# Scores of two heads at once in row tiles, several query blocks per group, in a two-network forward pass

## The chip, the cores and the metric

The kernel runs on one core of a Trainium2 chip. The metric is the device time of one execution in microseconds (us), as the median of several runs. Beside it there is one profiled execution, from which all durations come. Engines are named as in the profile: PE is TensorE's matmul, PEld its weight load, DVE is VectorE, ACT is ScalarE, POOL is GpSimd, SP issues most of the transfers; a "q" behind a name (SPq, ACTq) is the instruction queue of that engine.

## The reference, cut to what matters

A sequence of 512 tokens with 1024 features goes through two networks, one after the other. All data are fp32. Three attentions lie in it, each followed by an output projection and a feed-forward part:

```python
# 1. forgetting attention: 8 heads of 64 features
logits = einsum('bhqd,bhkd->bhqk', qf, kf) + c[q] - c[k]      # c: running sum of log gates
logits = where(key <= query, logits, -inf)                    # causal
# 2. differential attention: 8 heads, each with two maps over 64 features
sc = einsum('bqhcd,bkhcd->bhcqk', q, k) * scale
p = masked_softmax(sc, key // 64 <= query // 64)              # in chunks of 64
a = p[:, :, 0] - lam * p[:, :, 1]
# 3. latent attention: 16 heads, scores over 64 + 32 = 96 features
proj = h @ w_in                                               # 384 + 256 + 32 columns
sc = (einsum(q_nope, k_nope) + einsum(q_pe, k_pe)) * scale    # same chunk mask
```

## The kernel before

**Arithmetic.** Every fp32 operand is split into a high and a low part of type fp32r, and each product is three matmuls: high by high, low by high (or high by low), and the other. The weights stream from memory in chunks of up to 1024 columns per partition (`RAW`), are split by ACT (`WH`, L1990) and DVE (`WL`, L1809), and are used at once. A chunk feeds 12 to 24 matmuls.

**Order of the work.** The kernel is written as many small generators ("strands") that yield steps. A planner at build time gives each step an estimated duration (`takes`) and picks, engine by engine, the step that can begin first, with some patience for more urgent ones. The order it finds is fixed in the program; on the chip each engine runs its own list and waits on semaphores. So a change of the estimates or of the steps can move work on every engine. PSUM has eight banks; `cap["gemm"]` and `cap["one"]` say how many of them projections and attention steps may hold.

**Scores.** A query block is 128 queries; block i sees (i + 1) * 128 keys. In the forgetting attention ("fg") and the latent attention ("mla") one step `score` computes one head and one block in one bank: three matmuls over the keys (L1747 to L1749), for "fg" a fourth one that adds the gates (L1752), and one of 128 columns that adds the mask in the last 128 keys (L1753, operands in `RC`). In "fg" two heads lie in one 128-row tile of Q, rows 0 to 63 and rows 64 to 127. The step uses all 128 rows: the keys of a head stand in their own tile of `KT` whose other half was zeroed at the start (`k_zero`, L2121). In "mla" the matmuls over the keys use 96 rows, the mask matmul all 128:

```python
mask = (IDR, MASK_C) if kind == "fg" else (HALF, MASK_H)
...
e.matmul(dst[:, nk - P:nk], *st.mask, start=False, stop=True)   # L1753
```

In the differential attention ("da") one step `score_two` computes the two maps of one head and one block in two banks. Its matmuls use 64 rows each, rows 0 to 63 for one map and rows 64 to 127 for the other, in turn (L1761), and two mask matmuls of 64 rows (L1763). After each score come `max` (DVE, L1870), `exp` (ACT, L2068), the division (DVE, L1876 or its "da" form), the transposes on PE (`turn`, L1664), their split into `PT` (ACT L1994, DVE L1815), and one `value` step per head (L1659 to L1661).

**Gates of "fg".** `gate_rows` issues four small transfers on SP (L1635), from `R` to `FS`, which place the eight heads' gate rows on partitions; ACT then copies them (`gate_cq`, L2086) and makes a selected row set for each head (`key_row`, L2064). On SP the next weight chunk stands behind these transfers (L1596).

**Latent projection.** `w_in` of the latent attention has 672 columns. They are computed in two passes over eight k-tiles and four token tiles, of 512 and 160 columns (L1688 to L1690).

Of the kernel before, what the change touches and what calls it, by code (L numbers as in the profile page):

```python
# [5 lines left out]
P = 128  # L6
S = 512
# [12 lines left out]
C_ID, C_MA, C_MC, C_IH, C_ONE = 0, 128, 256, 384, 512  # L20
C_SEL = 640
C_BASE = 648
C_CDA, C_SDA = 650, 682
C_CML, C_SML = 714, 778
C_WF = 842
C_END = 906
# [7 lines left out]
STN = 8  # L34
# [9 lines left out]
    "vec": {"pe": 1, "act": 1}, "cvec": {"pe": 1, "act": 1}, "consts": {"act": 1}, "k_zero": {"pool": 1}, "blank": {"pool": 1},  # L44
# [5 lines left out]
    "key_row": {"act": 1}, "score": {"pe": 1}, "score_two": {"pe": 1}, "max": {"dve": 1}, "exp": {"act": 1},  # L50
# [87 lines left out]
def takes(kind, eng, f):  # L138
# [9 lines left out]
    if eng == "pe":  # L148
# [48 lines left out]
    return {"acc": 1595.0, "window": 1250.0, "kpe_copy": 1130.0, "k_zero": 520.0, "ramp": 220.0}.get(kind, 120.0)  # L197


def build(nc, a, out):  # L200
    with ExitStack() as ctx:
# [11 lines left out]
        RC = sb("RC", [P, 512], F32R)  # L213
# [17 lines left out]

        IDR, MASK_C, MASK_H, HALF = (RC[:, n * P:n * P + P] for n in range(4))

# [22 lines left out]
        strands, ready_at, free_at = [], {}, dict.fromkeys(LAG, 0.0)  # L256
# [7 lines left out]
        def emit(kind, **fields):  # L264
            t = None
            for eng, n in SIGNALS[kind].items():
# [33 lines left out]
        def run():  # L300
            while strands:
# [22 lines left out]
                s = min((x for x in can if x[1] == eng and x[0] <= t + PATIENCE[eng]), key=lambda x: x[2].rank)[2]  # L324
# [402 lines left out]
        def landing(s, t):  # L727
# [7 lines left out]
        k_zeros = [emit("k_zero", lo=64 if hh % 2 == 0 else 0, i=s * 8 + hh * 2 + x).pool  # L735
                   for s in range(2) for hh in range(4) for x in range(2)]
        kfree = [[k_zeros[-1]] for _ in range(16)]
# [105 lines left out]
        def k_tiles(base):  # L843
            def put(n, bank, done):
                parts, his = [(base + (2 * n + x) * 2, slice(64 * x, 64 * x + 64)) for x in (0, 1)], []
                for i, r in parts:
                    st = yield step("hi", dst=KT[r, i, :], src=bank[r, :], scale=1.0, after=counts([done, kfree[i], kfree[i + 1]]))
                    his.append(st.act)
                for (i, r), hi in zip(parts, his):
                    st = yield step("lo", dst=KT[r, i + 1, :], src=bank[r, :], high=KT[r, i, :], scale=None, from_x=False, after=[hi])  # L850
                    kready[i] = [st.dve]
                return [st.dve]
            return put

# [10 lines left out]
        def attention(groups, kind, lag):  # L865
            nh = 2 if kind == "da" else 4
            krows = 96 if kind == "mla" else P
            mask = (IDR, MASK_C) if kind == "fg" else (HALF, MASK_H)
            units = [(G, h, i) for G in groups for h in range(nh) for i in range(4)]
# [4 lines left out]
            def key_rows(G, h, u):  # L874
                while u > state.scored + 2 or not (flags.consts and G.gated) or not tiles.fr:
                    yield None
# [1344 lines left out]
```

## Time and profile before

| | |
|---|---|
| runs | 1829.54, 1827.6, 1829.36 us; median 1829.36 us |
| the profiled execution, its own time | 1828.21 us |
| its span (first to last instruction) | 1826.4 us |
| granted TensorE clock, mean | 1.00 |
| PE busy | 1808.6 us (99%) |
| PEld busy | 1494.4 us (82%) |
| DVE busy | 1121.5 us (61%) |
| ACT busy | 799.3 us (44%) |
| POOL busy | 145.2 us (8%) |

The duration of a matmul in the profile is from its start to its modelled end, and matmuls overlap in it; what one costs in a stream is the distance to the start of the next one. "Idle before" counts only time in which no record of the engine is open. The forgetting attention lies at about 68 to 150 us of the span, the differential one at 618 to 800 us, the latent projection and attention at 1220 to 1440 us; the rest is projections and feed-forward parts.

### The profile page before, as it was taken

The numbers are of one execution on the slowest core, as the hardware profiler recorded it, in microseconds if no ns is written. First come the engines' busy times: TensorE is split into PE (matmuls) and PEld (weight loads), VectorE is DVE, ScalarE is ACT, GpSimd is POOL, SyncE is SP. The second block draws the span as 40 slices with busy tenths as digits, with TensorE's granted clock in tenths as the row PEclk, the third lists the DMA queues.
The fourth block names the chain that finished last, engine by engine and source line by source line (L and its number), as shares of the span: only waits on it lengthen the run. The fifth ranks groups of instructions, "written<-read, shape, count | busy, mean of one in ns | idle before, by whom it ended". The sixth has DMA issues, their size and how long they took to land.

```text
span 1826.4 us, 23160 instructions
## 1 busy us (share of the span) xinstructions
PE 1808.6 (99%) x8960; PEld 1494.4 (82%) x8960; DVE 1121.5 (61%) x1898; ACT 799.3 (44%) x1426; POOL 145.2 (8%) x149
## 2 busy tenths in 40 slices
PE   9999999999999999999999999999999999999998
PEld 7898788888888888888888888779888888888886
DVE  5577644344345777696754654655989776366375
ACT  6562432122235455544432433447766544144144
POOL 4003200000004100002000000024000100000000
PEclk9999999999999999999999999999999999999999
DMA  5212323322332211213323333222011233332331
GB/s 160 71 36 67 105 92 93 92 93 93 100 96 92 70 59 61 68 58 93 93 93 92 93 93 99 92 79 73 26 58 36 59 93 97 99 93 93 92 117 68
DMA packets 128251, 152.24 MB, mean 83 GB/s; under 512 B 9291, under 2 KB 100973, under 8 KB 128141
## 3 DMA queue, kind: packets, MB, share of 16 engines
q1 hardware_dynamic: 127980, 150.69, 26.8%
q8 instruction: 71, 1.16, 0.3%
q14 instruction: 40, 0.32, 0.1%
q10 hardware_dynamic: 160, 0.07, 0.0%
HBM read 148.56 MB, written 2.10 MB: 82 GB/s over the span
## 4 chain that ended last, share of the span: by engine, by line
PE 92%; DVE 3%; issue 1%; ACT 1%; POOL 1%; DMA 0%; SPq 0%; DVEq 0%; POOLq 0%; ACTq 0%
PE bk L1659 22%; PE bk L1661 22%; PE bk L1660 22%; PE bk L1688 6%; PE bk L1689 5%; PE bk L1690 5%; PE bk L1664 4%; PE bk L1761 1%; PE bk L1747 1%; PE bk L1749 1%; PE bk L1748 1%; PE bk L1726 1%; DVE XT L1821 1%; PE bk L1733 1%; POOL FS L2130 1%
## 5 line engine op out<-in xcount | busy, mean ns | idle before, releaser
L1659 PE MATMUL bk<-R,WH 128*128 128x512 f32 x1764 | 700.6, 397 | 1.8 <-DVE R L1799 1.3
L1660 PE MATMUL bk<-R,WH 128*128 128x512 f32 x1764 | 696.7, 395 | 0.0
L1661 PE MATMUL bk<-R,WL 128*128 128x512 f32 x1764 | 696.7, 395 | 0.0
L1809 DVE TENSOR_TENSOR WL<-RAW,WH 128x1024 fp32r<-128x1024 f32 (+4 forms) x277 | 341.1, 1232 | 529.3 <-ACT WH L1990 527.8
L1990 ACT ACTIVATE WH<-RAW 128x1024 fp32r<-128x1024 f32 (+4 forms) x277 | 287.9, 1039 | 651.6 <-PE bk L1661 593.0
L1659 PEld LDWEIGHTS bk<-R,WH 128*128 128x128 f32 x1764 | 330.8, 188 | 81.7 <-issue 2.9
L1661 PEld LDWEIGHTS bk<-R,WL 128*128 128x128 f32 x1764 | 330.6, 187 | 80.9
L1660 PEld LDWEIGHTS bk<-R,WH 128*128 128x128 f32 x1764 | 330.8, 188 | 78.7
L1688 PE MATMUL bk<-WH,R 128*128 128x512 f32 (+4 forms) x528 | 187.8, 356 | 0.0
L1689 PE MATMUL bk<-WH,R 128*128 128x512 f32 (+4 forms) x528 | 180.2, 341 | 0.0
L1690 PE MATMUL bk<-WL,R 128*128 128x512 f32 (+4 forms) x528 | 180.1, 341 | 0.0
L2130 POOL TENSOR_TENSOR FS<-FS 128x512 f32<-128x512 f32 x49 | 75.4, 1549 | 910.0 <-ACT FS L2014 908.2
L1799 DVE SCALAR_TENSOR_TENSOR FS<-FS,VEC 128x511 f32<-128x511 f32 (+1 forms) x176 | 125.1, 747 | 7.8 <-ACT FS L2096 7.0
L1821 DVE TENSOR_TENSOR XT<-bk,XT 128x512 f32<-128x512 f32 x152 | 100.8, 684 | 25.7 <-PE bk L1661 25.4
L1688 PEld LDWEIGHTS bk<-WH,R 128*128 128x128 f32 x528 | 99.7, 189 | 11.4 <-issue 1.0
L1690 PEld LDWEIGHTS bk<-WL,R 128*128 128x128 f32 x528 | 99.4, 188 | 11.5
L1689 PEld LDWEIGHTS bk<-WH,R 128*128 128x128 f32 x528 | 99.7, 189 | 9.2
L2068 ACT ACTIVATE FS<-bk,SM 128x128 f32<-128x128 f32 (+3 forms) x160 | 83.5, 526 | 52.6 <-DVE SM L1870 52.1
L1910 DVE TENSOR_TENSOR FS<-bk,FS 128x512 f32<-128x512 f32 x136 | 90.2, 685 | 11.1 <-PE bk L1661 9.6
L2096 ACT ACTIVATE FS<-FS,VEC 128x512 f32<-128x512 f32 x88 | 69.0, 810 | 52.7 <-DVE FS L1910 52.7
L1870 DVE TENSOR_REDUCE SM<-bk 128x1 f32<-128x128 f32 (+3 forms) x160 | 72.8, 482 | 6.0 <-PE bk L1753 5.0
L1994 ACT ACTIVATE R<-FS 128x512 fp32r<-128x512 f32 x78 | 47.5, 623 | 63.4 <-DVE FS L1922 43.1
(153 smaller groups left out, 1676.3 us busy)
## 6 DMA issues: line engine op xcount, KB each, us to landing
RAW<-in_ffn_w_up_dram SPq DMA_DIRECT2D x176, 256.0 KB, 3.1
RAW<-in_ffn_w_down_dram SPq DMA_DIRECT2D x44, 512.0 KB, 3.7
RAW<-in_w_gate_dram SPq DMA_DIRECT2D x44, 256.0 KB, 2.9
RAW<-in_w_up_dram SPq DMA_DIRECT2D x44, 256.0 KB, 3.1
RAW<-in_w_down_dram SPq DMA_DIRECT2D x22, 512.0 KB, 3.6
RAW<-in_da_w_qkv_dram SPq DMA_DIRECT2D x32, 256.0 KB, 3.0
RAW<-in_w_out_dram SPq DMA_DIRECT2D x8, 512.0 KB, 3.7
RAW<-in_da_w_qkv_dram SPq DMA_DIRECT2D x8, 512.0 KB, 3.5
```

The costliest lines, as they stand in the source:

```text
L1659: e.matmul(dst, lh, rh, start=start, stop=False)
L1660: e.matmul(dst, lh, rl, start=False, stop=False)
L1661: return e.matmul(dst, ll, rh, start=False, stop=stop)
L1688: e.matmul(dst, R[:, xh, t], wh[:, j, :], start=st.start and j == 0, stop=False)
L1689: e.matmul(dst, R[:, xl, t], wh[:, j, :], start=False, stop=False)
L1690: mm = e.matmul(dst, R[:, xh, t], wl[:, j, :], start=False, stop=st.stop and j == top)
L1799: return e.scalar_tensor_tensor(out=dst, in0=x, scalar=s, in1=y, op0=o0, op1=o1)
L1809: e.tensor_tensor(low, RAW[:, r, 0:m], high.bitcast(F32), ALU.subtract).then_inc(on["wlo_dve"], 1)
L1821: e.tensor_tensor(XT[:, st.m, :], BK[st.bank][:, :], XT[:, st.m, :], ALU.add).then_inc(on["add_dve"], 1)
L1910: e.tensor_tensor(st.dst, BK[st.bank][:, :], st.bc, ALU.mult).then_inc(on["scaled_dve"], 1)
L1990: e.activation(home(st.n)[0], RAW[:, r, 0:m], ACT.Copy).then_inc(on["whi_act"], 1)
L2130: e.tensor_tensor(st.acc, st.acc, st.x, ALU.add).then_inc(on["acc_pool"], 1)
```

## The change

1. **One step `pair` replaces `score` of "fg" and `score_two` of "da".** It handles two heads of "fg" (or two maps of a "da" head) and one or more query blocks. All its matmuls use 64 rows, the two halves in turn, each into its own bank. In "fg" the keys of two heads now share one tile, as in "da" (`k_pair` instead of `k_tiles`), so the zeroing of `KT` is gone.
2. **Several blocks in one step** (`bundles`). In "fg" blocks 0 and 1 share a step and a bank per half, blocks 2 and 3 are steps of their own. In "da" blocks 0 and 1 likewise, and blocks 2 and 3 are one step with four banks.
3. **Masks.** `RC` holds `MASK_C`, `MASK_H` and a shifted identity that is read as `UPPER` and `LOWER`. In "fg" the causal mask needs two matmuls per half (one of 128 and one of 64 columns) instead of one. In "mla" the mask matmul uses rows 0 to 63 alone, where it used 128.
4. **Gates.** `gate_rows` issues eight transfers instead of four, since the gate rows are wanted on both halves; `key_row` runs once per pair of heads.
5. **The planner** adds 195 ns to an estimate where PE goes from `pair` to anything else or back, and prefers a further `pair` step right after one. Nothing is added for the mask of "mla".
6. **Latent projection** in passes of 384 and 288 columns; the transposes of its first three tiles wait for the first pass alone.
7. **Banks in "da"**: `cap["gemm"]` is 4 instead of 5. The lag of "da" (how many blocks the scores may be ahead) is 2 instead of 3.

The core of the diff:

```diff
-        if kind == "score":
-            return (3 if f["gate"] is None else 4) * mm((f["i"] + 1) * P) + 62
-        if kind == "score_two":
-            return 3 * max(220.0, 1.1 * mm((f["i"] + 1) * P)) + 200
+        if kind == "score":
+            return 3 * mm((f["i"] + 1) * P) + 62
+        if kind == "pair":
+            return sum((3 if f["gate"] is None else 4) * mm((i + 1) * P) + (60 if f["gate"] is None else 120) for i, _, _ in f["parts"])
...
+                    if eng == "pe" and (kind == "pair") != tiled[0]:
+                        t += 195.0
+                        tiled[0] = kind == "pair"
...
-            chunk(2, 512, (0, wap(m_in, k * P, 2, 0, 512)))
-        for k in (0, 4):
-            chunk(4, 160, (0, wap(m_in, k * P, 4, 512, 160)))
+            chunk(2, 384, (0, wap(m_in, k * P, 2, 0, 384)))
+        for k, n in ((0, 3), (3, 3), (6, 2)):
+            chunk(n, 288, (0, wap(m_in, k * P, n, 384, 288)))
...
-        k_zeros = [emit("k_zero", lo=64 if hh % 2 == 0 else 0, i=s * 8 + hh * 2 + x).pool
-                   for s in range(2) for hh in range(4) for x in range(2)]
...
-            attention([A0, A1], "fg", 2)
+            paired([A0, A1], "fg", 2, ([[0, 1]], [[2]], [[3]]))
...
-            cap["gemm"] = 5
-            attention(Gs, "da", 3)
+            cap["gemm"], cap["one"] = 4, 4
+            paired(Gs, "da", 2, ([[0, 1]], [[2], [3]]))
...
                     for r0, src, dst in st.rows:
                         e.dma_start(FS[r0:29 + r0:4, dst, 0:S], R[0:8, src, :].bitcast(F32)).then_inc(s_c, 16)
+                        e.dma_start(FS[64 + r0:93 + r0:4, dst, 0:S], R[0:8, src, :].bitcast(F32)).then_inc(s_c, 16)
...
-                    e.matmul(dst[:, nk - P:nk], *st.mask, start=False, stop=True).then_inc(on["score_pe"], 1)
+                    e.matmul(dst[:, nk - P:nk], UPPER[0:64, :], MASK_H[0:64, :], start=False, stop=True).then_inc(on["score_pe"], 1)
+                elif k == "pair":
+                    sides = (slice(0, 64), slice(64, 128))
+                    for i, o, bs in st.parts:
+                        nk, q = (i + 1) * P, slice(i * P, i * P + P)
+                        two = [(r, BK[b][:, o:o + nk]) for r, b in zip(sides, bs)]
+                        for x, y in ((0, 0), (1, 0), (0, 1)):
+                            for r, dst in two:
+                                e.matmul(dst, R[r, st.q[x], q], KT[r, st.kidx + y, 0:nk], start=x == y, stop=False)
+                        if st.gate is None:
+                            for r, dst in two:
+                                mm = e.matmul(dst[:, nk - P:nk], UPPER[r, :], MASK_H[r, :], start=False, stop=True)
+                        else:
+                            cq, ck = st.gate
+                            for r, dst in two:
+                                e.matmul(dst, R[r, cq, q], R[r, ck, 0:nk], start=False, stop=False)
+                            for r, dst in two:
+                                e.matmul(dst[:, nk - P:nk], UPPER[r, :], MASK_C[r, :], start=False, stop=False)
+                            for r, dst in two:
+                                mm = e.matmul(dst[:, nk - 64:nk], LOWER[r, :], MASK_C[r, 0:64], start=False, stop=True)
```

**Where the change moves instructions.** On PE the first scores of "fg" stand behind the same projection matmuls as before. Before (L1747 to L1749 keys, L1752 gates, L1753 mask, all of 128 rows; "128x128" is output partitions by columns):

```order
L1690 MATMUL bk5<-WL,R 128x512
L1747 MATMUL bk4<-KT,R 128x128 [waits key_row_act,gate_cq_act,tok_f_act,lo_dve]
L1748 MATMUL bk4<-KT,R 128x128
L1749 MATMUL bk4<-KT,R 128x128
L1752 MATMUL bk4<-R 128x128
L1753 MATMUL bk4<-RC 128x128
L1747 MATMUL bk1<-KT,R 128x256 [waits tok_f_act,lo_dve]
```

The same place now (L1848 keys, L1855 gates, L1857 and L1859 masks, all of 64 rows):

```order
L1778 MATMUL bk5<-WL,R 128x512
L1848 MATMUL bk4<-KT,R 128x128 [waits tok_f_act,key_row_act,lo_dve,gate_cq_act]
L1848 MATMUL bk1<-KT,R 128x128
L1848 MATMUL bk4<-KT,R 128x128
L1848 MATMUL bk1<-KT,R 128x128
L1848 MATMUL bk4<-KT,R 128x128
L1848 MATMUL bk1<-KT,R 128x128
L1855 MATMUL bk4<-R 128x128
L1855 MATMUL bk1<-R 128x128
L1857 MATMUL bk4<-RC 128x128
L1857 MATMUL bk1<-RC 128x128
L1859 MATMUL bk4<-RC 128x64
```

Two heads are computed where one was, and the first of these matmuls waits for the same two ACT steps. On PE in the latent attention, one block before (L1688 to L1690 are projection matmuls):

```order
L1747 MATMUL bk2<-KT,R 128x256 [waits lo_dve]
L1748 MATMUL bk2<-KT,R 128x256
L1749 MATMUL bk2<-KT,R 128x256
L1753 MATMUL bk2<-RC 128x128
L1688 MATMUL bk6<-WH,R 128x512 [waits lo_dve,tok_k_act]
```

and the first two blocks of a head now (L1835 to L1837 keys with 96 rows, L1838 mask with 64 rows):

```order
L1778 MATMUL bk6<-WL,R 128x384
L1835 MATMUL bk5<-KT,R 128x128 [waits lo_dve]
L1836 MATMUL bk5<-KT,R 128x128
L1837 MATMUL bk5<-KT,R 128x128
L1838 MATMUL bk5<-RC 128x128
L1835 MATMUL bk1<-KT,R 128x256 [waits lo_dve]
L1836 MATMUL bk1<-KT,R 128x256
L1837 MATMUL bk1<-KT,R 128x256
L1838 MATMUL bk1<-RC 128x128
```

A mask matmul still closes each block, 64 times in all, each between matmuls of 96 or 128 rows. On SP, where the gate rows are placed, before:

```order
L1596 DMA RAW<-in_w_in_dram 128x4x256 [waits wlo_dve]
L1635 DMA FS<-R 8x512 [waits gate_base_dve,lo_dve]
L1635 DMA FS<-R 8x512 x3
L1596 DMA RAW<-in_w_in_dram 128x4x256 [waits wlo_dve]
```

and now:

```order
L1683 DMA RAW<-in_w_in_dram 128x4x256 [waits wlo_dve]
L1722 DMA FS<-R 8x512 [waits gate_base_dve,lo_dve]
L1723 DMA FS<-R 8x512
L1722 DMA FS<-R 8x512
L1723 DMA FS<-R 8x512
L1722 DMA FS<-R 8x512
L1723 DMA FS<-R 8x512
L1722 DMA FS<-R 8x512
L1723 DMA FS<-R 8x512
L1683 DMA RAW<-in_w_in_dram 128x4x256 [waits wlo_dve]
```

Four transfers have come in ahead of the next weight chunk and of what ACT waits for.

Counted over the whole order of PE, unbroken runs of 64-row matmuls number 24 before, all in "da". Now there are 16 in "da", 10 in "fg" (two of the twelve steps follow another one directly) and 64 in "mla", these of one matmul each.

## Rows read from the trace of the kernel before

**Rows 1.** The page: span and busy time of PE.

```profile
span 1826.4 us, 23160 instructions
...
PE 1808.6 (99%) x8960; PEld 1494.4 (82%) x8960; DVE 1121.5 (61%) x1898; ACT 799.3 (44%) x1426; POOL 145.2 (8%) x149
```

**Rows 2.** Busy time by engine, first half of the latent attention; PEclk is the granted clock.

```profile
1262.00:1345.00 83.00, 79.98 (x497) 70.47 (x496) 71.47 (x171) 55.78 (x144) 14.19 (x20) 1.00 0.13 39
```

**Rows 3.** PE in order of time (start us, us), projections of 264 and 512 columns.

```profile
51.23 0.28 PE L1689 MATMUL bk<-WH,R 128*128 128x264 f32 x1
51.34 0.28 PE L1690 MATMUL bk<-WL,R 128*128 128x264 f32 x1
51.47 0.40 PE L1688 MATMUL bk<-WH,R 128*128 128x512 f32 x1
51.70 0.40 PE L1689 MATMUL bk<-WH,R 128*128 128x512 f32 x1
```

**Rows 4.** PE in order of time, latent projection, pass of 160 columns.

```profile
1233.82 0.27 PE L1689 MATMUL bk<-WH,R 128*128 128x160 f32 x1
1233.93 0.28 PE L1690 MATMUL bk<-WL,R 128*128 128x160 f32 x1
```

**Rows 5.** PE in order of time, a score of the forgetting attention: gates, mask.

```profile
73.19 0.27 PE L1752 MATMUL bk<-R 128*128 128x128 f32 x1
73.30 0.28 PE L1753 MATMUL bk<-RC 128*128 128x128 f32 x1
```

**Rows 6.** PE in order of time, differential attention: into and out of 64 rows.

```profile
618.28 0.28 PE L1689 MATMUL bk<-WH,R 128*128 128x256 f32 x1
618.40 0.28 PE L1690 MATMUL bk<-WL,R 128*128 128x256 f32 x1
618.65 0.55 PE L1761 MATMUL bk<-KT,R 64*128 64x128 f32 x6
...
619.52 0.26 PE L1763 MATMUL bk<-RC 64*128 64x128 f32 x2
619.71 0.39 PE L1688 MATMUL bk<-WH,R 128*128 128x256 f32 x1
619.94 0.28 PE L1689 MATMUL bk<-WH,R 128*128 128x256 f32 x1
```

**Rows 7.** Weight loads in order of time at the same place.

```profile
618.62 0.44 PEld L1761 LDWEIGHTS bk<-KT,R 64*128 64x128 f32 x6
...
619.71 0.19 PEld L1688 LDWEIGHTS bk<-WH,R 128*128 128x128 f32 x1
619.82 0.19 PEld L1689 LDWEIGHTS bk<-WH,R 128*128 128x128 f32 x1
```

**Rows 8.** PE in order of time, latent attention: a mask, then a block of 384.

```profile
1298.12 0.22 PE L1753 MATMUL bk<-RC 128*128 128x128 f32 x1
...
1298.41 0.34 PE L1748 MATMUL bk<-KT,R 96*128 96x384 f32 x1
1298.59 0.34 PE L1749 MATMUL bk<-KT,R 96*128 96x384 f32 x1
```

**Rows 9.** Weight loads at the same place: the two behind that mask's.

```profile
1298.13 0.19 PEld L1747 LDWEIGHTS bk<-KT,R 96*128 96x128 f32 x1
1298.24 0.19 PEld L1748 LDWEIGHTS bk<-KT,R 96*128 96x128 f32 x1
```

**Rows 10.** SP's queue in order of time: the gate rows.

```profile
60.31 2.75 SPq L1635 DMA_DIRECT2D FS<-R  x4
```

**Rows 11.** ACT in order of time: gate copy, weight split, key rows.

```profile
64.46 0.63 ACT L2086 ACTIVATE R<-FS 128x512 fp32r<-128x512 f32 x1 [3.62 <-DMA FS<-R]
65.38 1.06 ACT L1990 ACTIVATE WH<-RAW 128x1024 fp32r<-128x1024 f32 x1 [0.29 <-PE bk L1690]
66.34 1.32 ACT L2064 ACTIVATE R<-FS,CN 128x512 fp32r<-128x512 f32 x2
```

**Rows 12.** PE in order of time: the first score of all.

```profile
67.92 0.22 PE L1747 MATMUL bk<-KT,R 128*128 128x128 f32 x1
```

More of the change, by code:

```diff
@@ L323, in run @@
                 t, eng, _ = min(can, key=lambda x: (x[0], x[2].rank))
-                s = min((x for x in can if x[1] == eng and x[0] <= t + PATIENCE[eng]), key=lambda x: x[2].rank)[2]
+                more = [x for x in can if eng == "pe" and tiled[0] and x[2].next[0] == "pair" and x[0] <= t + 200.0]
+                s = min(more or (x for x in can if x[1] == eng and x[0] <= t + PATIENCE[eng]), key=lambda x: x[2].rank)[2]
                 kind, fields = s.next
@@ L841, in k_pair @@
             return put
[L843 to L853, printed above, removed]
         def k_tiles64(base):
@@ L870, in attention @@
+        def attention(groups, lag):
+            units = [(G, h, i) for G in groups for h in range(4) for i in range(4)]
             state = Group()
@@ L872, in attention, with unit @@
             state.halves = {}
-            def key_rows(G, h, u):
-                while u > state.scored + 2 or not (flags.consts and G.gated) or not tiles.fr:
-                    yield None
-                ck = tiles.get()
-                st = yield step("key_row", dst=R[:, ck.i, :], src=G.ck, head=G.h0 + h, after=counts([ck.free, G.ck_done]))
-                ck.ready = [st.act]
-                G.ckh[h] = ck
-            def one_map(L, u, c, b, scored):
+            def unit(u):
                 G, h, i = units[u]
                 nk, o = (i + 1) * P, u % STN * 8
-                nm, z = ST[:, o + c:o + c + 1], ST[:, o + 2 + c:o + 3 + c]
-                mx = yield step("max", dst=nm, src=BK[b.i][:, 0:nk], after=[scored])
+                while state.scored < u or u > state.turned + lag or not (G.turned and flags.consts and h < G.heads):
+                    yield None
+                nm, z, rz = (ST[:, o + x:o + x + 1] for x in (0, 2, 4))
+                b = yield from bank()
+                q, kidx = G.Q[h], G.kbase + 2 * h
+                st = yield step("score", bank=b.i, q=(q.h.i, q.l.i), kidx=kidx, i=i, rows=96,
+                                after=counts([b.free, q.ready, kready[kidx]]))
+                state.scored = u + 1
+                if i == 3:
+                    drop(q, st.pe)
+                mx = yield step("max", dst=nm, src=BK[b.i][:, 0:nk], after=[st.pe])
                 p = yield from fslot()
@@ L942, in unit @@
+                st = yield step("p_one", z=z, rz=rz, p=FS[:, p.i, 0:nk], after=[ex.act])
                 odd = h % 2
@@ L976, in values @@
                         drop(v, st.pe)
[L977 to L1006 removed]
+                yield from half_out(G, pair, odd, b, st.pe)
             for G in groups:
[L1009 to L1012 removed]
+                G.undone = 4
             for n in range(len(units) // 4):
@@ L1333, in turn_lat @@
             b = yield from bank()
-            st = yield step("heads", bank=b.i, c0=f * P, width=P, after=counts([b.free, lat.toks[0:4 if f < 4 else 8]]))
+            st = yield step("heads", bank=b.i, c0=f * P, width=P, after=counts([b.free, lat.toks[n - 4:n]]))
             lat.ups.append(st.pe)
```

352 lines of the change are left out of this document (207 added, 145 removed).

## The prediction

> **What bounds the kernel now.** I read the page first: PE is busy 1808.6 of 1826.4 us, and no other engine comes near [rows 1]. So the time is the length of PE's list plus its waits, and almost every edit has to be priced in PE time. A matmul's duration says little for that, since matmuls overlap; I read in the timeline of PE how far apart the starts of two neighbours are, and call it the slot. It is 0.23 us for 512 columns and 0.12 for 264 [rows 3], 0.12 for 256 [rows 6], 0.18 for 384 (0.175 over many) [rows 8], and 0.11 for 160 [rows 4] and for 128 [rows 5]. So below some 250 columns a slot is 0.11 us whatever its columns: the weight load takes that long. The clock granted is 1.00 (the 2.4 GHz level) [rows 2], and the slots hold at it.
>
> Second, the places where 64-row matmuls begin and end, since the change makes more of them. In an unbroken stream the next weight load starts together with the running matmul: behind the mask that starts at 1298.12 it starts at 1298.13 [rows 8, 9]. At 618.40 a 256-column matmul starts, the last of 128 rows; its stream is over 0.12 later, at 618.52. The first 64-row load starts only at 618.62 [rows 6, 7]. At the other end the last 64-row mask starts at 619.56 (a pair, the second 0.04 behind the 619.52), streams for 0.06 until 619.62, and the next 128-row load starts at 619.71, 0.09 later; its matmul is recorded with 0.39 us instead of 0.28 and its neighbour starts 0.23 behind it instead of 0.12. So at each crossing PE runs empty (0.10 and 0.09) and then shows the whole load (0.11). In: 0.21 us. Out: 0.20 us. As a check, from 618.40 to 619.94 are 1.54 us; the slots in it are two of 256 columns (0.24), five pairs at 0.11 and three at 0.12 (0.91): 1.15, and 0.39 is left for one way in and out.
>
> Third, what a pair costs. With 0.41 us for the two crossings by the loads, the eight pairs between them get 0.89, 0.11 each: a pair costs what a single matmul of its columns costs.
>
> **The change part by part, in PE time.**
>
> *Forgetting attention.* Before, a head is four blocks of four matmuls and a mask: 5 x 0.11, 4 x 0.12 + 0.11, 4 x 0.175 + 0.11, 4 x 0.233 + 0.11, together 3.0 us, 23.9 for eight heads. Now four pairs of heads: blocks of four pairs and two mask pairs, 0.67 + 0.69 + 0.92 + 1.15 = 3.4 us, 13.7 in all, and ten runs of 64 rows at 0.39: 17.6. Saved: 6.3 us.
>
> *Differential attention.* The same matmuls, but 16 runs for 24: 8 x 0.39 = 3.1 us saved.
>
> *Latent projection.* 96 matmuls of 512 and 96 of 160 become 96 of 384 and 96 of 288. 288 lies between 264 (0.12) and 384 (0.175), by a straight line at 0.132. Saved per pair 0.233 + 0.112 - 0.175 - 0.132 = 0.038, times 96: 3.6 us.
>
> *Masks of the latent attention.* This edit looks like nothing, and I take it for the largest. There are 64 of them, each now a single 64-row matmul between 96- or 128-row ones. From the end of the stream ahead to the start of the next matmul it takes in (0.21), stream (0.06), out (0.20): 0.47 us. Now it takes one slot of 0.11: load to load 1298.13 to 1298.24 [rows 9]. So 0.35 more, times 64: 22.4 us lost. The trace has no single one, so both ends: if the loads could still run ahead and only the emptying stays, 0.10 + 0.06 + 0.09 - 0.11 = 0.14 (9 us); if a single one costs its slot and the full 0.39, 25 us. Nothing at all is a rival below. I take 0.35, since in [rows 6, 7] both halves of the price show at both crossings.
>
> On this, the Trainium skill, TensorEngine Tiling (Array Packing), Key Properties, says that changing the tiling mode, not just the tile, drains TensorE. It gives no number; the gaps of 0.10 and 0.09 in [rows 7] agree with it, and the exposed load is what the trace adds. It speaks against this edit. Another page would have it the other way: the Trainium skill, TensorE: Matmul & The Clock Gate, Step-by-step: what each phase is for, has weight loads pulled ahead of running matmuls where they go to the background buffer. By it the masks would cost nothing and the sum would be 22 us lower, as in rival one.
>
> *Gates.* Four transfers are issued in 2.75 us [rows 10]; eight take 2.7 us more. ACT waits for them (3.62 us idle already), then splits a weight chunk and makes the key rows [rows 11]: the first is done 0.66 after 66.34, at 67.00. PE reads it at 67.92 [rows 12], after the same matmuls as now. The 2.7 us shrink by the 0.29 that ACT then waited for PE; the first key row comes at 69.4, and PE stands still for 1.5 us. Behind it in PE's list is all the rest. Ends: 1.0 and 2.5. The weight chunk behind the transfers on SP comes 2.7 us late too; a chunk feeds 24 matmuls of 0.233, 5.6 us, and three are split ahead, so it costs nothing; without that cover it would add up to 2.7.
>
> *At nothing:* the zeroing of the keys (POOL, at the very start, long before a key tile is read); fewer key splits on ACT and DVE in the first attention (both have idle time there); one bank less for projections in the differential part (a bank is read out while three others still compute; uncovered it would be one copy of 0.63 us as in [rows 11] for each of eight projections, 5 us).
>
> *What is absorbed.* In 1262 to 1345 PE is idle 3.0 of 83 us while DVE is busy 71.5 [rows 2]. Idle counts only what exceeds the 0.28 us tail of the last matmul, so up to twice that is waiting. There half the masks lie, and PE's longer list gives DVE the time it lacked. I take 3 us, between 0 and 6.
>
> **Sum.** -6.3 - 3.1 - 3.6 + 22.4 + 1.5 - 3.0 = +7.9 us against the profiled execution: its span would be 1834.3 and its own time 1836.1. The median of the runs stands 1.15 above that execution's own 1828.21, so I predict 1837 for the median.
>
> **The rivals.** 0.2% is 3.7 us, about what a measurement can tell from no change.
>
> *One: a single 64-row matmul at rows 0 to 63 crosses free.* Then only the savings and the gate stall are left: -13.0 + 1.5 = -11.5, 1818 us, faster. For it: no such matmul is in the trace. Against it: every crossing there is shows both parts. It decides the sign when a mask costs under (11.5 - 3)/64 = 0.13 us, with nothing absorbed under 0.18. Chance 0.11.
>
> *Two: a part of the price.* The loads run ahead (0.14 each, 9 us) or the absorption is at its end of 6 us: 9 - 11.5 = -2.5 in the one case, 22.4 - 11.5 - 6 = +4.9 in the other; between them 1826 to 1833. For it: DVE at 86% busy in half the masks' stretch. Against: an absorption of 6 needs twice the waiting that the rows show. Chance 0.14, of it 0.04 faster and 0.10 the same.
>
> *Three: bursts that starve.* A two-group step of the differential part needs all four attention banks at once, and a transpose behind it waits until an exp gives one back; the scores are now ahead by two blocks instead of three. Eight such steps, each late by one copy of 0.63 us [rows 11], add 5 us to the forecast: 1842. Against: projections stand between the steps in the order. Chance 0.07.
>
> *The forecast,* the masks at about 0.35: 0.68, its own range 1833 to 1843 (0.30 to 0.39 a mask, the absorption 0 to 6).
>
> **How the numbers follow.** Forecast, two and three together hold 0.89, and the range 1826 to 1844 covers about 0.8 of the whole; rival one lies outside. Faster: 0.11 + 0.04 = 0.15. Same: 0.10 of rival two and 0.03 of the forecast's lower end, 0.13. Slower: the rest, 0.72.
>
> **What would show it.** In the trace of the changed kernel: around each latent mask (L1838) its weight load should start 0.1 us after the stream ahead is over, not with it, and the next matmul's load about 0.25 us after the mask's, with a duration 0.1 longer; if the loads stay 0.11 apart, rival one holds. The stretch of the latent attention should be some 19 us longer, the first one 5 us shorter with its gate stall, the differential one 3 shorter, and the first `pair` should start near 69.4 with PE idle before it. PE's total idle should stay under 20 us; if it grows by 5 in the differential part, rival three holds. The prediction fails if a mask costs under 0.2 us, or if the new order makes waits that the old trace can't show.

## The result: 1.0% faster, where 0.4% slower was predicted

| | median of the runs | lowest to highest |
|---|---|---|
| before, run beside it | 1829.45 us (4 runs) | 1827.6 to 1830.07 |
| changed kernel | 1811.14 us (4 runs) | 1809.0 to 1812.49 |

The ratio is 0.9901, 95% interval 0.9883 to 0.9918. The predicted 1837 us and its range (1826 to 1844) lie above it. One execution of one kernel below (everything 32 bytes on) fell into a slower state, 1969.9 us at a granted clock of 0.85, and is left out of its median.

The page of the changed kernel, for [rows 1]:

```profile
span 1810.7 us, 23164 instructions
...
PE 1785.5 (99%) x8992; PEld 1496.8 (83%) x8992; DVE 1120.2 (62%) x1895; ACT 791.7 (44%) x1419; POOL 136.1 (8%) x133
```

PE is busy 23.1 us less, but it has 32 matmuls more, and it stands idle 25.2 us where it was 17.8 (the prediction wanted under 20 as a sign). So the time came from matmuls that cost less, not from fewer waits. To see which, I looked first where the change does nothing. Between 300 and 400 us of the span there are only feed-forward matmuls of 512 columns, before and after. These are the windows of PE there (stretch, length, busy and number of matmuls, granted clock, DMA share, GB/s), of the kernel before:

```profile
300.00:400.00 100.00, 100.00 (x430) 1.00 0.31 94
```

and of the changed one:

```profile
300.00:400.00 100.00, 100.00 (x442) 1.00 0.33 98
```

The same clock, no idle time, and 12 matmuls more in 100 us. PE in order of time shows it from matmul to matmul (start, duration in us), before:

```profile
299.95 0.39 PE L1660 MATMUL bk<-R,WH 128*128 128x512 f32 x1
300.18 0.40 PE L1661 MATMUL bk<-R,WL 128*128 128x512 f32 x1
300.42 0.39 PE L1659 MATMUL bk<-R,WH 128*128 128x512 f32 x1
300.65 0.40 PE L1660 MATMUL bk<-R,WH 128*128 128x512 f32 x1
```

and after:

```profile
300.05 0.39 PE L1748 MATMUL bk<-R,WH 128*128 128x512 f32 x1
300.27 0.39 PE L1749 MATMUL bk<-R,WL 128*128 128x512 f32 x1
300.50 0.39 PE L1747 MATMUL bk<-R,WH 128*128 128x512 f32 x1
300.73 0.39 PE L1748 MATMUL bk<-R,WH 128*128 128x512 f32 x1
```

Three slots took 0.70 us and take 0.68. Over the 100 us (one of the counted matmuls reaches in from before) that is 0.2331 and 0.2268 us a slot. The kernel has three groups of 1764 matmuls of 512 columns that read `R` and the weights (`WH` or `WL`), 5292 in all, so 5292 x 0.0063 = 33 us. The prediction had counted this slot as fixed.

**What the change itself did** can be read where the prediction said. A mask of the latent attention, in PE's order of time:

```profile
1245.86 0.28 PE L1837 MATMUL bk<-KT,R 96*128 96x256 f32 x1
1246.07 0.32 PE L1838 MATMUL bk<-RC 64*128 64x128 f32 x1
1246.32 0.44 PE L1835 MATMUL bk<-KT,R 96*128 96x384 f32 x1
1246.60 0.33 PE L1836 MATMUL bk<-KT,R 96*128 96x384 f32 x1
```

The weight loads at the same place:

```profile
1245.74 0.19 PEld L1837 LDWEIGHTS bk<-KT,R 96*128 96x128 f32 x1
1246.07 0.18 PEld L1838 LDWEIGHTS bk<-RC 64*128 64x128 f32 x1
1246.32 0.19 PEld L1835 LDWEIGHTS bk<-KT,R 96*128 96x128 f32 x1
```

The stream of the 256 columns is over at 1245.98, the mask's load starts 0.09 later (forecast 0.1), the next load 0.25 behind that one (forecast 0.25), and the matmul behind it is recorded with 0.44 instead of 0.34 [rows 8]. From 1245.86 to 1246.60 are 0.74 us. With a mask that costs its slot it would be 0.12 + 0.11 + 0.175 = 0.405, so the mask costs 0.335 more, times 64: 21.4 us (predicted 22.4).

The gates of the forgetting attention, in PE's order:

```profile
67.27 0.39 PE L1778 MATMUL bk<-WL,R 128*128 128x512 f32 x1
69.34 0.55 PE L1848 MATMUL bk<-KT,R 64*128 64x128 f32 x6 [1.69 <-ACT R L2160]
```

and the first and last of the eight transfers on SP's queue:

```profile
60.14 0.74 SPq L1722 DMA_DIRECT2D FS<-R  x1
...
64.93 0.62 SPq L1723 DMA_DIRECT2D FS<-R  x1
```

They end at 65.55, 2.5 us behind the four of [rows 10] (63.06), and the first pair starts at 69.34 (predicted 69.4) with PE idle for 1.69 us (predicted 1.5). Against [rows 12] that is 1.42 us later.

**Two things are new in this trace.** The waits of PE by line and releaser (us in total, times, longest), the costliest ones:

```profile
PE bk L1747 <- DVE R L1911: 3.1, 2, 2.3
PE bk L1752 <- ACT TOK L2146: 2.6, 1, 2.6
PE bk L1747 <- DVE R L1895: 2.2, 2, 2.0
```

And three stretches in which the granted clock is at its lower level, 1.2 GHz. One of them, in windows of PE:

```profile
575.00:578.00 3.00, 2.05 (x14) 1.00 0.41 140
578.00:585.00 7.00, 7.00 (x22) 0.51 0.24 75
```

The same in order of time:

```profile
577.01 2.49 PE L1814 MATMUL bk<-CN,FS 128*128 128x1 f32 x16 [0.95 <-POOL FS L2223]
...
579.93 0.63 PE L1777 MATMUL bk<-WH,R 128*128 128x512 f32 x1
580.36 0.63 PE L1778 MATMUL bk<-WL,R 128*128 128x512 f32 x1
```

PE had been idle for 0.95 us and then worked on sixteen matmuls of a single column; from 578 to 585 us the clock is 0.51 and matmuls of 512 columns start 0.43 us apart. The kernel before has 1.00 in the same windows. The two others lie at 816.9 us (behind an idle time of 2.26) and near 1301.8. They cost 3.4, 1.7 and 1.7 us (length times the missing share of the clock), 6.8 together. In the kernel before the granted clock is 1.00 up to its last 2 us.

### The profile page after: what moved, and what is told of

Read it like the earlier page. It is cut to its first block, busy times and chain, and to the rows that moved or that the text cites. A ratio compares the mean times of both kernels' runs of the same rounds, so it can differ in the third digit from the quotient of the medians.

```text
span 1810.7 us, 23164 instructions
## 1 busy us (share of the span) xinstructions
PE 1785.5 (99%) x8992; PEld 1496.8 (83%) x8992; DVE 1120.2 (62%) x1895; ACT 791.7 (44%) x1419; POOL 136.1 (8%) x133
## 4 chain that ended last, share of the span: by engine, by line
PE 91%; DVE 3%; ACT 2%; issue 2%; POOL 1%; DMA 0%; SPq 0%; DVEq 0%; POOLq 0%; ACTq 0%
PE bk L1747 22%; PE bk L1748 22%; PE bk L1749 22%; PE bk L1776 5%; PE bk L1778 5%; PE bk L1777 5%; PE bk L1752 4%; PE bk L1848 1%; PE bk L1838 1%; PE bk L1814 1%; POOL FS L2223 1%; DVE XT L1917 1%; PE bk L1835 1%; PE bk L1821 1%; PE bk L1836 1%
## 5 line engine op out<-in xcount | busy, mean ns | idle before, releaser
L1747 PE MATMUL bk<-R,WH 128*128 128x512 f32 x1764 | 693.2, 393 | 5.6 <-DVE R L1911 3.1
L1749 PE MATMUL bk<-R,WL 128*128 128x512 f32 x1764 | 688.6, 390 | 0.0
L1748 PE MATMUL bk<-R,WH 128*128 128x512 f32 x1764 | 688.3, 390 | 0.0
L1747 PEld LDWEIGHTS bk<-R,WH 128*128 128x128 f32 x1764 | 332.1, 188 | 75.0 <-issue 6.2
L1749 PEld LDWEIGHTS bk<-R,WL 128*128 128x128 f32 x1764 | 332.0, 188 | 69.7
L1966 DVE TENSOR_REDUCE SM<-bk 128x1 f32<-128x128 f32 (+3 forms) x160 | 71.2, 482 | 12.6 <-PE bk L1838 6.1
```

What stands on the lines that cost most here:

```text
L1747: e.matmul(dst, lh, rh, start=start, stop=False)
L1748: e.matmul(dst, lh, rl, start=False, stop=False)
L1749: return e.matmul(dst, ll, rh, start=False, stop=stop)
```

## Experiments: where the slot comes from

**Theory.** The change makes `RC` 64 columns narrower (256 bytes of a partition) and `CN` 60 columns wider (240 bytes). Tensors lie one behind the other, at starts that are rounded to 32 bytes, so all that lies behind `RC` moves down by 32 bytes against the weights. `R`, the other operand of nearly all matmuls, began 61728 bytes behind `WH`, and begins 61696 bytes behind it now. The lines that do it:

```diff
-C_END = 906
+C_END = 966
...
-        RC = sb("RC", [P, 512], F32R)
+        RC = sb("RC", [P, 448], F32R)
```

The theory: the distance of the two operands sets the slot. Rival A: something in the changed order (DMA, DVE, POOL) makes PE's stream faster. Rival B: not the distance counts but where `R` itself begins. All kernels below ran beside the kernel before on the same chip; its medians there were 1829.5 to 1830.1 us, so a comparison across the sections can be off by 0.6 us.

**Kernel before, 32 bytes more.** Only an unused tensor is added:

```diff
         RC = sb("RC", [P, 512], F32R)
+        PAD = sb("PAD", [P, 8], F32)
         VEC = sb("VEC", [P, V_END], F32)
```

> The kernel before with nothing but an unused tensor of 32 bytes per partition ahead of VEC, so that R, KT, PT and FS begin at a multiple of 64 bytes of their partition, as they do in the changed kernel (in the kernel before they begin 32 bytes past one). No instruction and no order changes. Theory A, placement: the 512-column slot of the projections falls from 0.2333 us to 0.2267 as in the changed kernel, some 6350 slots x 0.0066 = 42 us less PE time, partly given back in waits at stage borders, where PE is now ahead of the others: 1785 to 1800 us. Theory B, the new order of the instructions or less traffic by the other engines made the slots shorter: nothing changes, 1829 us and 0.2333.

Measured: 1807.11 us, ratio 0.9879 (0.9865 to 0.9892). An unused tensor is worth more than the whole change. Its windows:

```profile
300.00:400.00 100.00, 100.00 (x439) 1.00 0.31 95
```

439, a slot of 0.228, not quite that of the changed kernel, and the time lies above the 1785 to 1800 us that were expected. Rival A has fallen: no instruction and no order changed. But a start at a multiple of 64 bytes isn't the whole rule.

**Changed kernel, the old distance** (the same line added there, so that `R` is 61728 bytes from `WH` again).

> The changed kernel with an unused tensor of 32 bytes ahead of VEC, so that R, KT, PT and FS begin 32 bytes past a multiple of 64, as in the kernel before. No instruction changes. Theory A: the slot goes back to 0.2333 and the time is that of the change alone, which my sum puts 8 us over the kernel before: 1833 to 1841 us. Theory B: 1811 us and 0.2267.

Measured: 1842.71 us, ratio 1.0073 (1.0059 to 1.0087):

```profile
300.00:400.00 100.00, 100.00 (x430) 1.00 0.30 95
```

With the old slot back, the change makes the kernel slower, by 12.6 us.

**Changed kernel, everything 32 bytes on** (the unused tensor stands ahead of `XT`, the first of all: `R` and `WH` both move, their distance does not).

> The changed kernel with an unused tensor of 32 bytes ahead of everything, so that the split weights (WH, WL) and the activations (R, KT, PT) all begin 32 bytes past a multiple of 64; the distance of R from WH is a multiple of 128 bytes, as in the changed kernel, where both begin at one. Theory A1, the distance of the two operands of a matmul modulo 128 counts: slots of 0.227 us, 1811 us. Theory A2, the place of R alone counts: 0.2333 as with R moved alone, about 1842 us.

Measured: 1812.23 us, ratio 0.9908 (0.9893 to 0.9923), as the changed kernel. Rival B has fallen, by the time alone; the slot of this kernel isn't read.

**Changed kernel, weights moved instead of `R`** (32 bytes ahead of `WH` and `WL`, 32 more ahead of `VEC`: `R` moves by 64, the distance is 61728).

> The changed kernel with WH and WL 32 bytes further and R, KT and PT 64 bytes further, so R begins at a multiple of 64 bytes as in the kernel before with 32 bytes added (slot 0.229), but stands 32 modulo 128 from WH, as in the kernel before (slot 0.2333). Theory A1: 0.2333 and about 1842 us. Theory A2: 0.229 and about 1825 us.

Measured: 1841.87 us, ratio 1.0065 (1.0053 to 1.0078), and 430 matmuls in the window. That is the time of the second kernel of this section (1842.71): two ways to the same distance give the same time. And `R` begins here where it does in the first one (1807.11), so its own start doesn't set the slot.

**Kernel before, 96 bytes more** (the unused tensor of the first experiment with 24 columns).

> The kernel before with an unused tensor of 96 bytes ahead of VEC: R begins 0 modulo 128 from WH, as in the changed kernel. By theory A1 its slot is 0.227 us, 0.0065 less than before over some 6350 slots, 41 us less PE time; some 10 us of it may come back in waits and clock at stage borders: 1788 to 1800 us. It is also the fair partner of the changed kernel: the difference between them is the worth of the change without the placement, which I put at +8 and which the pair with R at 32 gave as +12.6.

Measured: 1823.68 us, ratio 0.9968 (0.9956 to 0.998):

```profile
300.00:400.00 100.00, 100.00 (x432) 1.00 0.30 94
```

1788 to 1800 us were expected. So a distance that is a multiple of 128 bytes isn't enough, and my rule was wrong. What fits all runs so far is the distance modulo 256: 61824 is 128 there.

**Kernel before, 224 bytes more,** to test that rule where it predicts and to give the changed kernel a fair partner (56 columns, distance 61952, 0 modulo 256).

> The kernel before with one edit, an unused tensor of 224 bytes per partition ahead of VEC, so that R begins 61952 bytes behind WH, 0 modulo 256 like in the changed kernel. Theory, the distance modulo 256 sets the slot: slot of 512 columns 0.227 us instead of 0.233 as in the changed kernel, and a time under the 1807 of the kernel with 64 bytes, near 1795 to 1805, if the engines behind PE keep up; then the changed kernel's own edits cost 6 to 16 us at equal placement. Rival, it is not the distance but the size of the shift (32 bytes less was good, 32 more was good, 96 more was not): then 0.233 and 1829 again. Second rival, distance counts modulo 512 (the changed kernel's 61696 is 256 modulo 512, this one's is 0): then any slot but 0.227.

Measured: 1796.03 us, ratio 0.9828 (0.9814 to 0.9841):

```profile
300.00:400.00 100.00, 100.00 (x443) 1.00 0.31 96
```

The rule held where it was tried, and both its rivals fell: 61696 and 61952 differ by 256 and give the same slot. That pair alone shows the period.

| distance R - WH, modulo 256 | kernels | matmuls in 300 to 400 us | median, us |
|---|---|---|---|
| 0 | changed; before + 224 bytes | 442; 443 | 1811.14; 1796.03 |
| 32 | before; changed + 32 bytes | 430; 430 | 1829.45; 1842.71 |
| 64 | before + 32 bytes | 439 | 1807.11 |
| 128 | before + 96 bytes | 432 | 1823.68 |

**The same within one trace.** Behind `R` lie `KT` and `PT`, and their distances to it are multiples of 256 bytes in every kernel here. The kernel before keeps the weights of its last projection there. PE in order of time:

```profile
1789.80 0.39 PE L1689 MATMUL bk<-KT,R 128*128 128x512 f32 x1
1790.03 0.39 PE L1690 MATMUL bk<-KT,R 128*128 128x512 f32 x1
1790.26 0.39 PE L1688 MATMUL bk<-KT,R 128*128 128x512 f32 x1
1790.48 0.39 PE L1689 MATMUL bk<-KT,R 128*128 128x512 f32 x1
```

Three slots take 0.68 us here, as in the changed kernel, where `WH` and `R` take 0.70 in this same kernel. Over the whole trace the median distance between two neighbours is 227 ns for `KT` with `R` (76 of them) and 234 for `R` with `WH` (1731). In the changed kernel both are 227, and with 32 bytes more there (where `R` moves and `KT` with it) they are 227 and 234 again. So it is the pair of tensors that counts, within one kernel too.

The distance table also tells what the change is worth. At distance 32 it costs 12.6 us (against the kernel before in the same section) to 13.3 us (by the table's medians), at distance 0 it costs 15.1. The placement gives 33.4 us to the kernel before and 31.6 to the changed one.

## Experiments: the parts of the change

**The mask alone, in the kernel before** (rows 0 to 63 in the latent attention, nothing else).

```diff
-                    e.matmul(dst[:, nk - P:nk], *st.mask, start=False, stop=True).then_inc(on["score_pe"], 1)
+                    mask = st.mask if st.rows == P else tuple(m[0:64, :] for m in st.mask)
+                    e.matmul(dst[:, nk - P:nk], *mask, start=False, stop=True).then_inc(on["score_pe"], 1)
```

> The kernel before with one edit of the change alone: the mask matmul of the latent attention on rows 0 to 63. By the sum +22 us of PE time less up to 6 us that the waits of that stretch absorb: 1845 to 1852 us. If the price is only the emptying, 0.14 us each: 1832 to 1838.

Measured: 1846.56 us, ratio 1.0096 (1.0082 to 1.011), 16.5 us more.

**The changed kernel with the old mask:**

```diff
-                    e.matmul(dst[:, nk - P:nk], UPPER[0:64, :], MASK_H[0:64, :], start=False, stop=True).then_inc(on["score_pe"], 1)
+                    e.matmul(dst[:, nk - P:nk], UPPER, MASK_H, start=False, stop=True).then_inc(on["score_pe"], 1)
```

> The changed kernel with the mask matmul of the latent attention on 128 rows again (the same sum twice over: the masked places get a number twice as far below, the others none). By the sum 64 masks at 0.35 us are 22 us of PE time, so 1789 us, or up to 8 us more where PE then waits for the others instead. If a single 64-row matmul were cheap in truth and the loads seen around it were only recorded late: 1811, no change.

Measured: 1794.95 us, ratio 0.981 (0.9797 to 0.9824), 16.2 us less than the changed kernel. This one edit taken back makes a faster kernel than the change was.

**All but the mask, at the old distance** (the last edit and the 32 bytes).

> The changed kernel with the latent mask on 128 rows and 32 unused bytes ahead of VEC, so that R is 61728 bytes from WH (32 modulo 256), as in the kernel before: all edits but the mask's, at the old placement. The prediction's sum without masks and absorption is -6.3 - 3.1 - 3.6 + 1.5 = -11.5: about 1818. Rival, from the runs so far: grouping blocks gave 3 us where 6 were reckoned, and the changed kernel at this distance was 12.6 over the kernel before where the mask alone gave 16.5, so the other edits together give only 4 us: 1825. At 1825 the savings are eaten by new waits and half-clock stretches, at 1818 the masks cost more beside the other edits than alone.

Measured: 1823.03 us, ratio 0.9969 (0.9959 to 0.9979). The prediction's sum for this was 1818. Against the changed kernel at that distance (1842.71) the masks are worth 19.7 us here. The mask's line in that one (64 rows), weight loads and matmuls (count: shortest/median/longest in ns):

```profile
L1839 PEld LDWEIGHTS bk<-RC x64: 182/183/183, 1266.6 to 1437.6; 64*128 64x128 f32 x64
L1839 PE MATMUL bk<-RC x64: 322/324/326, 1266.6 to 1437.6; 64*128 64x128 f32 x64
```

and with 128 rows:

```profile
L1839 PEld LDWEIGHTS bk<-RC x64: 187/188/193, 1267.2 to 1420.8; 128*128 128x128 f32 x64
L1839 PE MATMUL bk<-RC x64: 222/226/278, 1267.2 to 1421.0; 128*128 128x128 f32 x64
```

From the first mask to the last are 171.0 us with 64 rows and 153.6 with 128 (the loads' rows), 17.4 us for the 64 of them, and not one of them is spared: the shortest matmul is recorded with 322 ns. Before 32 of the 64 loads the load engine stood idle, 9.8 us in all, and the profile shows nothing that it waited for. Of the 21.4 us 4.0 were absorbed here.

**One block to a step** (in the changed kernel, 42 runs of 64-row matmuls in the first two attentions instead of 26).

```diff
-            paired([A0, A1], "fg", 2, ([[0, 1]], [[2]], [[3]]))
+            paired([A0, A1], "fg", 2, ([[0]], [[1]], [[2]], [[3]]))
...
-            paired(Gs, "da", 2, ([[0, 1]], [[2], [3]]))
+            paired(Gs, "da", 2, ([[0]], [[1]], [[2]], [[3]]))
```

> The changed kernel with one query block in each pair step, in both attentions; everything else, the placement too, stays. By the order PE then enters 64-row mode 14 times in the first attention instead of 10 and 28 times in the differential one instead of 16. At 0.39 us each way and back that is 6 us more: 1817 us. If the larger steps cost waits (rival three), some of it is won back: 1811 to 1814.

Measured: 1813.9 us, ratio 0.9918 (0.9906 to 0.9931), 2.8 more than the changed kernel, though the intervals of the two overlap. 16 runs at 0.39 would be 6.2.

**The passes of the latent projection alone, in the kernel before.**

```diff
-            yield from gemm_t(NM.X, 8, 512, ev_lat(NM, 0, 512))
-            yield from gemm_t(NM.X, 8, 160, ev_lat(NM, 512, 160))
+            yield from gemm_t(NM.X, 8, 384, ev_lat(NM, 0, 384))
+            yield from gemm_t(NM.X, 8, 288, ev_lat(NM, 384, 288))
```

> The kernel before with one edit, the latent projection in passes of 384 and 288 columns; the distance of R from WH stays 61728 bytes (32 modulo 256). Prediction's term: 96 times 0.233 + 0.112 - 0.175 - 0.132 = 3.6 us less, so about 1826. Rival: the shorter slots give PE less cover and it waits for DVE or ACT instead, then within 1 us of the kernel before, 1829.

Measured: 1829.53 us beside 1829.53 of the kernel before, ratio 1.0002 (0.9993 to 1.0011): nothing. Its waits of PE in the stretch:

```profile
PE bk L1666 <- ACT TOK L2052: 2.6, 1, 2.6
```

PE in order of time there:

```profile
1258.45 0.34 PE L1692 MATMUL bk<-WL,R 128*128 128x384 f32 x1
1261.36 3.05 PE L1666 MATMUL bk<-CN,TOK 128*64 128x128 f32 x14 [2.57 <-ACT TOK L2052]
```

And the window right behind:

```profile
1262.00:1266.00 4.00, 4.00 (x22) 0.64 0.21 53
```

The passes now have 384 and 288 columns. But behind a row of 384-column matmuls PE has nothing else to do until ACT has written `TOK` for the transposes, 2.57 us, and a stretch of the lower clock begins there (0.64 over 4 us, 1.4 us lost in these alone). Together that is 4.0 us, about the 3.6 that were to be saved.

**The changed kernel with the old mask and the old passes:**

> The changed kernel with the latent mask on 128 rows (1794.95 us so far) and, beside it, the latent projection in its old passes of 512 and 160 columns; R lies 61696 bytes from WH, 0 modulo 256. What is left of the change are the pairs and blocks of the first two attentions and the gates. By the prediction's term the passes were worth 3.6 us: 1798.5. By the run of the passes alone (1829.53 for 1829.53) they are worth nothing, since a wait of 2.6 us for ACT and a stretch at the 1.2 GHz level came with them: about 1795, and both of these should be gone from this trace.

Measured: 1792.64 us, ratio 0.9802 (0.9788 to 0.9815), 2.3 us under the one with the new passes (the intervals of the two overlap) and the lowest of all kernels here. The wait on `TOK` is gone from its trace. At equal placement (1796.03) the pairs, the blocks and the gates together give 3.4 us (the intervals only touch), where 6.3 + 3.1 - 1.5 = 7.9 were predicted (that this is the number of the forecast's sum is chance). Its trace has stretches of the lower clock too; two of them:

```profile
16.00:24.00 8.00, 6.15 (x23) 0.79 0.54 159
180.00:188.00 8.00, 6.91 (x23) 0.79 0.41 134
```

each 8 x 0.21 = 1.7 us. The first lies 50 us ahead of the first pair, where PE's list is the same as in the kernel before (the zeroing on POOL, now gone, lay in those first microseconds).

## Where the first two attentions' savings went

The starts of PE's key matmuls give a table by stage at equal placement. Two of the lines that read `KT` (shortest/median/longest in ns, first and last start), in the kernel before with 224 bytes more (its latent ones begin at 1247.67):

```profile
L1762 PE MATMUL bk<-KT,R x192: 268/332/501, 607.5 to 785.2; 64*128 64x128 f32 x48, 64*128 64x256 f32 x48, 64*128 64x384 f32 x48, 64*128 64x512 f32 x48
L1748 PE MATMUL bk<-KT,R x96: 220/365/499, 67.9 to 1400.8; 96*128 96x128 f32 x16, 96*128 96x256 f32 x16, 96*128 96x384 f32 x16, 96*128 96x512 f32 x16
```

and in the changed kernel (its differential ones begin at 604.49):

```profile
L1848 PE MATMUL bk<-KT,R x288: 268/331/503, 69.3 to 794.4; 64*128 64x128 f32 x36, 64*128 64x256 f32 x36, 64*128 64x384 f32 x36, 64*128 64x512 f32 x36
L1835 PE MATMUL bk<-KT,R x64: 224/387/501, 1244.8 to 1416.4; 96*128 96x128 f32 x16, 96*128 96x256 f32 x16, 96*128 96x384 f32 x16, 96*128 96x512 f32 x16
```

| from, to | before + 224 bytes | changed | difference | of it lower clock | predicted |
|---|---|---|---|---|---|
| start to first score | 67.9 | 69.3 | +1.4 | 0 | +1.5 |
| to first differential score | 539.6 | 535.2 | -4.4 | 3.4 | -6.3 |
| to first latent score | 640.2 | 640.3 | +0.1 | 1.7 | -3.1 - 3.6 |
| to last latent score | 153.1 | 171.6 | +18.5 | 1.7 | +22.4 - 3.0 |
| to the end | 392.8 | 394.3 | +1.5 | about 0 | 0 |

The start is as forecast. In the first attention's stage 1.9 us are missing, and the stretch of 0.51 over 7 us in it costs 3.4, so without it 7.8 us would be saved, more than the 6.3. In the third line 6.8 us are missing: 1.7 are the lower clock behind the wait at 816.9, and 4.9 are waits. The windows of PE there, in the changed kernel:

```profile
604.00:1245.00 641.00, 633.60 (x3341) 1.00 0.27 82
```

and in the kernel before with 224 bytes more:

```profile
607.00:1248.00 641.00, 638.46 (x3350) 1.00 0.27 82
```

PE is idle 7.4 us for 2.5. The large waits are the 2.3 us for DVE at 816.9 and the 2.6 us for `TOK`; the kernel with the old passes is without the second one. In the latent attention the difference without the lower clock is 16.8, where 19.4 was summed: more of the masks was absorbed. The +1.5 of the last line isn't explained.

During the differential scores themselves PE isn't starved, in the changed kernel (first line) as in the one before with 224 bytes more:

```profile
604.00:795.00 191.00, 189.63 (x1263) 1.00 0.20 62
607.00:786.00 179.00, 178.31 (x1200) 1.00 0.19 60
```

1.4 us idle in 191, and 0.7 in 179. So rival three (bursts that starve) didn't come. But the last of these scores now starts 189.9 us behind the first, where it was 177.7 us, and 22 us later PE waits for DVE at 816.9. Whether the smaller lag or the bank less does that wasn't tried.

**With the clock taken out.** Each run has the mean granted clock of its execution. Its span times that clock is an estimate of what it would have taken at full clock, good to 1 or 2 us: the clock has three digits (0.9 us), and a stretch of the lower clock in the last microseconds, when PE has little left to do, is counted too. The clocks are 0.998 or 0.999 in the median for the six kernels with the old steps, and 0.995 to 0.998 for the eight with pairs.

| compared | by the medians | at full clock | predicted |
|---|---|---|---|
| changed, for before, at distance 32 | +12.6 | +10.7 | +7.9 |
| changed, for before, at distance 0 | +15.1 | +10.0 | +7.9 |
| masks, in the kernel before | +16.5 | +17.0 | +19.4 |
| masks, in the changed kernel | +16.2 | +16.4 | +19.4 |
| masks, in the changed one at distance 32 | +19.7 | +16.7 | +19.4 |
| pairs, blocks and gates, at distance 0 | -3.4 | -8.2 | -7.9 |
| passes, in the kernel before | 0.0 | -1.3 | -3.6 |
| passes, in the changed kernel with the old mask | +2.3 | +1.8 | -3.6 |

So the three pairs of the masks agree to 0.6 us, and the saving of the first two attentions did come, in time at full clock; 4.8 us of it went into the lower clock.

## Why the prediction was wrong

**The step that failed** stands in its first part: the slot "is 0.23 us for 512 columns", with the clock at 1.00, "and the slots hold at it". I took 0.233 as what 512 columns cost. It is what they cost at this kernel's placement. The change moves `R` by 32 bytes against the weights, the slot became 0.227, and 5292 of them made some 33 us that no term of the sum had. The edit that does it, the width of `RC` and `CN`, stood in no part of the prediction, not even under "at nothing". The forecast's sign was right for the edits that it did weigh: at equal placement the changed kernel is slower, by 12.6 and 15.1 us, where +7.9 was summed. The second half of that step failed too, though by less: the clock wasn't 1.00 throughout in the changed kernel, which is 2 and 5 of these us, and 2 to 3 remain, the balance of the terms below; that they are so few is in part luck, since 4.9 us of waits that no term had stand against more saved in the first attention and more absorbed in the latent one.

**The masks** (+22.4, less 3.0 absorbed): right in each step of the mechanism, 21.4 by its own rows and 16.2, 16.5 and 19.7 by three pairs of runs, or 16.4 to 17.0 with the clock taken out. So 4 to 5 us were absorbed, where 3.0 was taken, within its bounds of 0 to 6. (By the prediction's own terms, 0.47 less 0.11, a mask costs 0.36 and not 0.35; that is 0.6 us in all.) Rival one (free) is refuted by all three pairs. The Trainium skill, TensorEngine Tiling (Array Packing), Key Properties, has the mode change drain TensorE; the trace agrees, with 0.09 us between the end of the stream and the mask's load in the rows above, and all 64 mask matmuls recorded alike (322 to 327 ns). The rule of the Trainium skill, TensorE: Matmul & The Clock Gate, Step-by-step: what each phase is for, that weight loads are pulled ahead of running matmuls, did not hold at these masks.

**Forgetting and differential attention** (-6.3 and -3.1): together with the gates 3.4 us were gained instead of 7.9, and 8.2 at full clock. The saving is there and is mostly given back in stretches of the lower clock. For the grouping of the blocks alone 2.8 us were measured where 6.2 were reckoned.

**Latent passes** (-3.6): nothing in the one kernel, and 2.3 us the other way in the other, where the intervals overlap. No saving came of this term: the passes change what stands ahead of the transposes, and I had not asked what PE would wait for there.

**Gates** (+1.5): 1.4, by the same chain as predicted.

**At nothing:** the bank less in the differential part made no idle time among the scores (1.4 us), but the scores end 12 us later and a wait of 2.3 follows, so it can't be called free. Neither it nor the zeroing was tried by itself.

**What stays open.** Which mechanism makes the distance count isn't shown, and only four of its values modulo 256 were tried. And I can't say how much of the lower clock is the change's. The kernels before with nothing, 32 and 224 bytes more show none of these stretches in their profiled execution until its last microseconds, the changed kernel and its variants show three or four each. But the kernel before with 96 bytes more has one as well, though no instruction of it differs:

```profile
592.34 1.92 PE L1727 MATMUL bk<-CN,FS 128*128 128x1 f32 x16 [0.47 <-POOL FS L2131]
...
596.00:600.00 4.00, 4.00 (x14) 0.70 0.04 12
```

Those near 596 us in the kernel before with the masks alone and with the passes alone lie ahead of all that was edited there. And the wait of 2.6 us for `TOK` is followed by one in some of these traces and not in the changed kernel's.

## What to carry to other kernels

Before a term is made of "the same matmul costs the same", look whether the change alters any tensor's size: here an unused tensor of 224 bytes gave 1.8%, more than the work on all three attentions. Compare a change with the kernel before at equal placement, or the placement's luck is taken for the change's merit. A 64-row matmul of 128 columns alone between others of 96 or 128 rows cost four times its slot here (0.445 us for 0.11), so half the rows of a short matmul are no saving. The lower clock took some 5 us more from one kernel than from another, so the granted clock of every run belongs beside its time. And a saving on PE counts only up to the next place where PE waits for another engine.

## What the runs showed of the hardware

- The slot of 512 columns (fp32r) at full clock depends on the distance between the two operands' tensors in a partition: 0.226 to 0.227 us (443 and 442 in 100 us) at 0 modulo 256, 0.228 (439) at 64, 0.232 (432) at 128, 0.233 (430) at 32. In all those windows the clock is 1.00, PE is never idle and the DMA share is 0.30 to 0.33. Other distances weren't tried.
- The Trainium skill, TensorE: Matmul & The Clock Gate, Step-by-step: what each phase is for, gives TensorE two independent SBUF read ports for the streamed and the loaded operand, so that a load takes no read bandwidth from the running matmul, and a gap of 216 ns for 512 columns. The runs here don't bear that out for fp32r: moving either operand against the other changes the gap, and the smallest is 226 to 227. What the two share isn't shown.
- A lone 64-row mask matmul between matmuls of 96 or 128 rows costs 0.335 us above its slot, and 16.4 to 17.0 us for 64 of them at full clock.
- Matmuls of 512 columns start 0.43 us apart at the lower clock level (1.2 GHz). Before one such stretch PE was idle 0.95 us and did sixteen one-column matmuls, before another it was idle 0.47 us and did the same, before a third it was idle 2.26 us, before a fourth 2.57.
